# GpSimd's rotation of the next tile and its scaling of head norms, placed behind the last level of a recurrence tile

## The chip, the cores and the metric

The kernel runs on one core of a Trainium2 chip. The core has TensorE (PE in the profile, its weight loads PEld), VectorE (DVE), ScalarE (ACT), GpSimd (POOL), SyncE (SP) and 16 DMA engines. The metric is the device time of one execution of the whole program in microseconds, as the median over runs. The kernel before takes 2104.66 us (median of 3 runs, 2103.86 to 2107.75).

## What is computed

Two layers of a hybrid encoder over 1040 frames of a new stream and 32 frames of a running one. Each layer normalises its input, projects it with `w_in` into twenty slices, runs four groups of heads, and merges them with gates and `w_out`. Two of the four groups, HGRN2 and retention, are the gated linear recurrence below; retention's queries and keys are first rotated, and both outputs are normalised per head. This is the part around the change:

```python
q_d = _rope(heads(dq, H_D), pos)
k_d = _rope(heads(dk, H_D), pos) * (HD_D ** -0.5)
...
# _gla: S_t = diag(exp(logf_t)) S_{t-1} + k_t v_t^T,  o_t = S_t^T q_t, block by block
b = jnp.cumsum(gb, axis=1)
inter = jnp.einsum('bthk,bhkv->bthv', qb * jnp.exp(b), S)
att = jnp.einsum('bthk,bshk,btshk->bhts', qb, kb, decay)
intra = jnp.einsum('bhts,bshv->bthv', att, vb)
S_new = jnp.exp(b_end)[..., None] * S + jnp.einsum('bshk,bshv->bhkv', kb * jnp.exp(b_end[:, None] - b), vb)
...
def _head_rms(o):
    return (of * lax.rsqrt(jnp.mean(of * of, axis=-1, keepdims=True) + EPS)).astype(o.dtype)
```

The other two groups are forgetting attention and sparse attention. For the sparse one a threshold per query is found by a bitwise search over index scores, which VectorE does in many small pieces while other stages run.

## The kernel before, in words

Frames are cut into nine tiles of 128 (tile 0 holds the running stream and the 16 meta tokens, tiles 1 to 8 the 1024 frames). A layer runs in four stages: index scores with the first projections, the recurrence, the rest of the projections, and attention with the output projection. The order on each engine is the order of the code, and engines meet by semaphores only.

The recurrence goes tile by tile. For tile t TensorE makes the cumulative sums of the log decays (L1031, L1032), turns queries and keys (L1036, L1038 for HGRN2; L1046 for retention, which waits for `x_rope`), and then goes through the levels (L1067): `ret`, 0, and 1 to 7 (1 to 5 in tile 0). A level from 1 on is a product of queries and keys weighted with decays of its block size, so for each level VectorE makes a difference of sums (`dl`, L1848), ScalarE its exponentials (L1548, L1549), VectorE multiplies keys and queries with them (L1887 and twice L1890, releasing `x_ql`), TensorE multiplies (releasing `x_lv`), and VectorE copies the result under a mask into `attA` (L1868, L1872, releasing `x_cp`). Behind the levels TensorE makes outputs (L1085, L1090) and state updates (L1098); VectorE adds them to the states (L1920, releasing `x_s`).

Projection work fills the gaps. Between the steps of a tile TensorE runs `fill` (L927, L924), a number of matmul steps laid down by `UPTO`, and 8 steps are one job. ScalarE empties a finished job's bank (L1414, releasing `p_ev`) and stores it (L1420); the job after the next one needs that bank. VectorE fills its own gaps with `search`: the counts at L1783, and after each eight counts the small operations L1822, L1824, L1826 and L1817. Fifteen such steps belong to each tile from 1 on: 8 before L1840, 2 before the levels, 5 behind them.

GpSimd per tile: `clear` (L2161, a memset of `attA`), `decayed` (L2145, L2146, L2149), `forget(t + 1)` (L2130, L2132, L2136), `rotate(t + 1)` (L2115, L2116, L2120, L2121, L2123, releasing `x_rope`), and `normed_heads(t - 1)` (L2156, releasing `x_on`). ScalarE waits for `x_on` in `store_heads(t - 1)` (L1504), which stands in its order behind the exponentials of the last level. Behind it in ScalarE's order come the evacuations of jobs that end late in the tile (L1414), the copy of the outputs (L1563) and the first steps of the next tile (L1521, L1522, L1523, releasing `x_eb`).

Of the kernel before, what the change touches and what calls it, by code (L numbers as in the profile page):

```python
# [31 lines left out]
NT = 1 + SEQ // P  # L32
# [121 lines left out]
def steps(keys):  # L154

    return {k: i + 1 for i, k in enumerate(keys)}
# [7 lines left out]
def one_more(count):  # L164

    count[0] += 1
    return 1


def encoder(nc, ins, outs, cf_d, cb_d, cm_d, cf_at, cb_at, cm_at):  # L170
# [10 lines left out]
    with ctx:  # L181
# [5 lines left out]
        def sem(name):  # L187
            s = ctx.enter_context(nc.semaphore(name))
            all_sems.append(s)
            return s  # L190
# [7 lines left out]
        def C(name):  # L198
            return cf[:, slice(*cf_at[name])]
# [273 lines left out]
        def span(mu):  # L473
            cols = [(c, w) for _, w, c in pieces_of(mu)]
            return min(c for c, _ in cols), max(c + n for c, n in cols)
# [111 lines left out]
        LEV = [(t, j) for t in T_all for j in (["ret", 0] + list(range(1, 6 if t == 0 else 8)))]  # L587
# [49 lines left out]
        x_cp, x_cp_at = sem("x_cp"), steps(LEV)  # L637
# [46 lines left out]
        for layer in range(DEPTH):  # L684
# [10 lines left out]
            with nc.Block() as block:  # L695
# [658 lines left out]
                def copy_keys(copy, a, own_sem, own):  # L1354

                    _, m, u, j = a
                    b = tbank[a]
                    if m == "fox":
                        rows = NS if u == "s" and j == NCACHE else P
                        col = (P * j if u == "s" else max(0, width(u - 1))) if u != 0 else 0  # L1360
                        n_ = HALF if u == 0 else rows
                        return copy(foxKT[0:HD + 1, :, col:col + n_], ps[0:HD + 1, 512 * b:512 * b + 512].rearrange("p (h n) -> p h n", h=H)[:, :, 0:n_])
                    if u == "s":
                        n_ = min(SW - P * j, 4 * P)
                        return copy(dsaKT["s"][0:HD, P * j:P * j + n_], ps[0:HD, 512 * b:512 * b + n_])
                    if j == 0:
                        copy(dsaKT["p"][0:HD, 0:HALF], ps[0:HD, 512 * b:512 * b + HALF]).then_inc(own_sem, one_more(own))
                        return copy(dsaKT["p"][0:HD, HALF:HALF + 3 * P], ps[0:HD, 512 * b + P:512 * b + 4 * P])
                    n_ = min(NT - j, 4) * P
                    return copy(dsaKT["p"][0:HD, width(j - 1):width(j - 1) + n_], ps[0:HD, 512 * b:512 * b + n_])  # L1370
# [729 lines left out]
                def _(pool):  # L2100
# [7 lines left out]
                    def rotate(t):  # L2108

                        pool.wait_ge(ld_mix[ld_mix_slot[t]], ld_mix_at[t] * 2)  # L2110
                        cosv = C("cos")[:, t * half:(t + 1) * half][:, None, :].broadcast_to([P, 4 * H, half])
                        sinv = C("sin")[:, t * half:(t + 1) * half][:, None, :].broadcast_to([P, 4 * H, half])
                        qk = LD[t % 2][:, 0:2, :].rearrange("p a (h d) -> p (a h) d", d=half)
                        rp = rope[t % 2]
                        G.tensor_tensor(rc.rearrange("p a b c -> p (a b) c"), qk, cosv, ALU.mult).then_inc(pool_own, one_more(own))  # L2115
                        G.tensor_tensor(rs_.rearrange("p a b c -> p (a b) c"), qk, sinv, ALU.mult).then_inc(pool_own, one_more(own))  # L2116
                        pool.wait_ge(pool_own, own[0])
                        if t >= 2:
                            pool.wait_ge(x_su, x_su_at[t - 2])
                        G.tensor_tensor(rp[:, :, 0], rc[:, :, 0], rs_[:, :, 1], ALU.subtract).then_inc(pool_own, one_more(own))  # L2120
                        G.tensor_tensor(rp[:, :, 1], rs_[:, :, 0], rc[:, :, 1], ALU.add).then_inc(pool_own, one_more(own))  # L2121
                        pool.wait_ge(pool_own, own[0])
                        G.tensor_tensor(kendD[t % 2].rearrange("p (h d) -> p h d", h=H), rp[:, H:].rearrange("p h a d -> p h (a d)"),  # L2123
                                        C("gk0" if t == 0 else "gk1")[:, :, None].broadcast_to([P, H, HD]), ALU.mult).then_inc(x_rope, 1)

                    def forget(t):

                        f = sig[t % 2]
                        pool.wait_ge(x_sg, x_sg_at[t])
                        G.tensor_tensor(f, f, oml[:, :], ALU.mult).then_inc(pool_own, one_more(own))  # L2130
                        pool.wait_ge(pool_own, own[0])
                        G.tensor_tensor(f, f, lb[:, :], ALU.add).then_inc(pool_own, one_more(own))  # L2132
                        pool.wait_ge(pool_own, own[0])
                        if t >= 2:
                            pool.wait_ge(x_qk, x_qk_at[t - 2])
                        G.tensor_scalar(kA[t % 2], f, -1.0, 1.0, ALU.mult, ALU.add).then_inc(x_kf, 1)  # L2136

                    def decayed(t):

                        if t >= 1:  # L2140
                            pool.wait_ge(x_su, x_su_at[t - 1])
                        pool.wait_ge(x_eb, x_eb_at[t])
                        pool.wait_ge(x_qke, x_qke_at[t])
                        pool.wait_ge(x_kf, x_kf_at[t])
                        G.tensor_tensor(QbA, QKA[:, 0], expb, ALU.mult).then_inc(pool_own, one_more(own))  # L2145
                        G.tensor_tensor(kendA, kA[t % 2], kex, ALU.mult).then_inc(pool_own, one_more(own))  # L2146
                        pool.wait_ge(x_qkde, 2 * x_qkde_at[t])
                        pool.wait_ge(pool_own, own[0])
                        G.tensor_tensor(QbD, QKD[:, 0], C("gq0" if t == 0 else "gq1"), ALU.mult).then_inc(x_qb, 1)  # L2149

                    def normed_heads(t):

                        pool.wait_ge(x_hr, x_hr_at[t])
                        if t >= 1:
                            pool.wait_ge(st_on, 16 * t)
                        G.tensor_tensor(oN, oAD, hr[:, :, None].broadcast_to([P, 2 * H, HD]), ALU.mult).then_inc(x_on, 1)  # L2156

                    def clear(t):
                        if t >= 1:
                            pool.wait_ge(x_o, x_o_at[t - 1])  # L2160
                        G.memset(attA, 0.0).then_inc(x_zero, 1)  # L2161
# [14 lines left out]
                    for t in T_all:  # L2176
                        if t >= 1:
                            clear(t)
                        decayed(t)
                        if t + 1 < NT:  # L2180
                            forget(t + 1)
                            rotate(t + 1)
                        if t >= 1:
                            normed_heads(t - 1)
# [82 lines left out]
```

## Time and profile before

| | us |
|---|---|
| median of 3 runs | 2104.66 |
| the profiled execution, whole | 2108.83 |
| its span | 2107.0 |
| PE busy in the span | 1923.3 (91%) |
| DVE busy | 1387.2 (66%) |
| ACT busy | 736.7 (35%) |
| POOL busy | 254.4 (12%) |
| mean granted TensorE clock | 0.988 |

The profile is of one execution, and its span is the time from the first to the last instruction. The recurrence stage lies at 231 to 532 us in the first layer and at 1282 to 1583 us in the second, and a tile of it takes 32 to 34 us. Idle time of an engine is printed before the instruction that ended it, in brackets, with the instruction that released it.

### The profile page before, as it was taken

The page shows a single profiled execution, that of the slowest core. Times are in us where ns is not written, and L with a number is a line of the kernel's source. Part 1 is how long each engine was busy: PE and PEld are TensorE (multiplying, and loading weights), DVE is VectorE, ACT ScalarE, POOL GpSimd, SP SyncE. Part 2 cuts the span into 40 slices and gives each one's busy share as a digit, 9 for nine tenths or more (in the row PEclk, how much of TensorE's full clock was granted, in tenths as well). Part 3 has the DMA queues.
Part 4 walks back from the last instruction along what each step waited for, and adds up shares of the span by engine and source line. Part 5 has one row for each costly group of instructions (what it writes and reads, how often), then busy time and mean ns, then how long its engine had stood idle before and what let it go on. Part 6 is the DMA issues. An engine that isn't in the chain of part 4 may idle for free. (4 is left out here: it accounts for less than half of the span.)

```text
span 2107.0 us, 27058 instructions
## 1 busy us (share of the span) xinstructions
PE 1923.3 (91%) x9670; PEld 1073.9 (51%) x9690; DVE 1387.2 (66%) x2961; ACT 736.7 (35%) x1678; POOL 254.4 (12%) x361
## 2 busy tenths in 40 slices
PE   7999999999998888999779999999999987889997
PEld 6434466555445556544364344665554455565443
DVE  4469398989796666542234693989888956674322
ACT  4451233423113444433244512434331134344332
POOL 0000223322100000001100002234221000000011
PEclk9999999999999999999979999999999999999999
DMA  7102232130513002224251022331314130122242
GB/s 245 59 22 78 70 106 86 61 103 28 154 38 73 14 14 91 87 99 147 107 175 61 23 75 75 103 99 46 103 43 139 38 76 11 34 70 88 99 149 105
DMA packets 151156, 173.44 MB, mean 82 GB/s; under 512 B 71392, under 2 KB 106848, under 8 KB 150832
## 3 DMA queue, kind: packets, MB, share of 16 engines
q1 hardware_dynamic: 122960, 134.34, 20.4%
q10 hardware_dynamic: 28064, 37.38, 5.0%
q8 instruction: 78, 1.28, 0.2%
q14 instruction: 54, 0.44, 0.1%
HBM read 114.94 MB, written 62.24 MB: 84 GB/s over the span
## 5 line engine op out<-in xcount | busy, mean ns | idle before, releaser
L927 PE MATMUL ps<-wring,xnT_arena 128*128 128x512 f32 (+2 forms) x2304 | 920.3, 541 | 0.0
L927 PEld LDWEIGHTS ps<-wring,xnT_arena 128*128 128x128 f32 x2304 | 403.1, 191 | 355.7 <-issue 338.7
L1783 DVE TENSOR_SCALAR_CACHE_REDUCE arena<-arena,theta 32x1056 bf16<-32x1056 f32 x496 | 461.3, 979 | 2.3
L1414 ACT COPY arena<-ps 128x512 f32<-128x512 f32 (+3 forms) x144 | 75.3, 523 | 447.7 <-PE ps L927 414.1
L1291 PE MATMUL ps<-wring,xnT_arena 128*128 128x512 f32 x512 | 222.8, 593 | 0.0
L2067 DVE TENSOR_REDUCE mneg<-ps 128x1 f32<-128x192 f32 (+9 forms) x148 | 113.9, 770 | 84.6 <-PE ps L1223 82.1
L1291 PEld LDWEIGHTS ps<-wring,xnT_arena 128*128 128x128 f32 x512 | 95.9, 190 | 114.8 <-issue 114.8
L1067 PEld LDWEIGHTS ps<-arena 128*128 128x128 f32 x488 | 68.7, 190 | 103.5 <-DVE arena L1890 75.1
L1067 PE MATMUL ps<-arena 128*128 128x128 f32 x488 | 79.5, 286 | 35.9 <-DVE arena L1890 35.7
L2235 POOL TENSOR_TENSOR arena<-arena 128x1024 f32<-128x1024 f32 (+1 forms) x16 | 35.4, 2213 | 584.0 <-DVE arena L2008 397.5
L1378 ACT COPY xnT_arena<-ps 128x512 f32<-128x512 f32 (+3 forms) x84 | 39.0, 464 | 181.8 <-PE ps L1235 139.1
L1221 PE MATMUL ps<-xnT_arena,arena 128*128 128x512 f32 (+4 forms) x240 | 86.3, 475 | 14.8 <-DVE xnT_arena L1378 13.2
L1221 PE MATMUL ps<-arena 128*128 128x512 f32 (+4 forms) x240 | 92.6, 473 | 7.8 <-DVE xnT_arena L1378 6.7
L1890 DVE TENSOR_TENSOR arena<-o_bc,arena 64x128 f32<-64x128 f32 x244 | 95.7, 392 | 3.8
L1645 ACT ACTIVATE arena<-ps,mneg 128x576 f32<-128x576 f32 (+5 forms) x84 | 80.9, 963 | 25.1 <-DVE mneg L2067 24.4
L1378 DVE COPY xnT_arena<-ps 128x512 f32<-128x512 f32 x104 | 61.2, 605 | 38.7 <-PE ps L1271 20.4
L1766 DVE SCALAR_TENSOR_TENSOR arena<-arena,iw 32x1056 f32<-32x1056 f32 (+7 forms) x64 | 63.7, 996 | 27.8 <-ACT arena L1477 25.7
L1235 PE MATMUL ps<-cf,arena 128*128 128x128 f32 (+2 forms) x596 | 79.1, 273 | 1.0 <-ACT arena L1645 1.0
L1872 DVE COPY_PREDICATED arena<-cm,ps 128x256 f32<-128x256 uint8 x122 | 63.5, 521 | 23.6 <-PE ps L1067 22.4
L1848 DVE TENSOR_TENSOR arena<-arena 128x256 f32<-128x256 f32 x122 | 76.2, 635 | 2.7
L1548 ACT ACTIVATE arena<-arena 128x128 f32<-128x128 f32 x122 | 37.7, 309 | 106.5 <-DVE arena L1848 100.1
L1235 PEld LDWEIGHTS ps<-cf,arena 128*128 128x128 f32 (+2 forms) x596 | 63.9, 136 | 18.9 <-issue 12.8
(271 smaller groups left out, 2468.0 us busy)
## 6 DMA issues: line engine op xcount, KB each, us to landing
projected<-arena ACTq DMA_DIRECT2D x130, 256.0 KB, 2.0
wring<-in_w_in SPq DMA_DIRECT2D x16, 1024.0 KB, 7.8
o_bc<-projected SPq DMA_DIRECT2D x36, 384.0 KB, 3.7
wring<-in_w_in SPq DMA_DIRECT2D x6, 2048.0 KB, 9.0
arena<-residual SPq DMA_DIRECT2D x17, 512.0 KB, 5.1
arena<-in_x_prompt SPq DMA_DIRECT2D x16, 512.0 KB, 5.0
wring<-in_w_out SPq DMA_DIRECT2D x8, 1024.0 KB, 6.1
residual<-arena SPq DMA_DIRECT2D x16, 512.0 KB, 2.7
```

The costliest lines, as they stand in the source:

```text
L927: o = mm(bank(pbank(k), 0, w_), xnT[:, c, t * P:(t + 1) * P], w, start=(c == 0), stop=(c == CH - 1))
L1067: o = mm(bank(level_bank(k), 2 * n_ * g, 2 * n_), keys[:, g * P:(g + 1) * P], queries[:, g].rearrange("p e n -> p (e n)"), start=True, sto ...
L1221: o = mm(ps[:, col:col + w], qt[:, h, :], kt[:, h if m == "fox" else 0, key:key + w], start=True, stop=not adds, skip_group_check=True)
L1235: o = tr(ps[0:w, 512 * tbank[a] + P * i:512 * tbank[a] + P * i + P], pbuf((m, u, h))[:, col:col + w], C("ident"))
L1291: o = mm(bank(OUT_BANK[t] + half), yT[t % 2][:, c, :], wring[:, c * D + 512 * half:c * D + 512 * half + 512], start=(c == 0), stop=(c == C ...
L1378: copy(ptile[pt_of[m, u, h]][:, 4 * g * P:4 * g * P + size], bank(tbank[a], 0, size)).then_inc(te, 1)
L1414: nc.scalar.copy(stage[s][:, 0:wide], bank(pbank(k), 0, wide)).then_inc(p_ev, 1)
L1645: A(pbuf((m, u, h))[:, 0:hi - lo], ps[:, base + lo:base + hi], ACT.Exp, bias=mneg[:, s:s + 1], accum_out=rsum[:, s:s + 1]).then_inc(a_exp, 1)
L1783: V.tensor_scalar(cmp_out[0][r, (i % 2) * WMAX:(i % 2) * WMAX + uw[u]], score[u][r], th_, 0.0, op, ALU.add, accum_out=into[r, i:i + 1]).th ...
L1848: V.tensor_tensor(dl[k[1] % 2].rearrange("p (b s) -> p b s", s=size), bv, bv[:, :, size // 2 - 1:size // 2].broadcast_to([P, 2 * P // size ...
L1890: V.tensor_tensor(QL[k[1] % 2][r, :, e, :].rearrange("p g (b i) -> p g b i", i=size // 2), cut_(QKA[:, 0])[r, :, :, size // 2:], cut_(E[k[ ...
L2067: V.tensor_reduce(mneg[:, s:s + 1], ps[:, base + lo:base + hi], X, ALU.max, negate=True).then_inc(a_max, 1)
```

## The change

One wait is added to GpSimd's program. Behind `forget(t + 1)` GpSimd waits until the last level's result of tile t has been copied (`x_cp`), and only then rotates tile t + 1 and scales the head norms of tile t - 1. The instructions and their order stay as they are.

```diff
                         decayed(t)
                         if t + 1 < NT:
                             forget(t + 1)
+                        pool.wait_ge(x_cp, x_cp_at[[k for k in LEV if k[0] == t][-1]])
+                        if t + 1 < NT:
                             rotate(t + 1)
                         if t >= 1:
                             normed_heads(t - 1)
```

GpSimd's instructions in tile 0, the first place where the wait stands, with the semaphores that each waits for (`-` is the kernel before, `+` the changed one):

```order
 L2132 TENSOR_TENSOR arena<-arena,lb 128x256 [waits pool_own]
 L2136 TENSOR_SCALAR arena<-arena 128x256 [waits pool_own]
-L2115 TENSOR_TENSOR arena<-o_bc,cf 128x512 [waits ld_mix1]
+L2115 TENSOR_TENSOR arena<-o_bc,cf 128x512 [waits ld_mix1,x_cp]
 L2116 TENSOR_TENSOR arena<-o_bc,cf 128x512
 L2120 TENSOR_TENSOR arena<-arena 128x8x32 [waits pool_own]
```

The first multiplication of `rotate` now waits for `x_cp` as well, and what follows it on GpSimd waits with it. In tile 8, where nothing is left to rotate, the wait stands before the scaling of tile 7's head norms; GpSimd's rows there in the changed kernel:

```order
L2145 TENSOR_TENSOR arena<-o_bc,arena 128x256 [waits x_qke,x_kf,x_eb,x_su]
L2146 TENSOR_TENSOR arena<-arena 128x256
L2149 TENSOR_TENSOR arena<-o_bc,cf 128x256 [waits pool_own,x_qkde]
L2156 TENSOR_TENSOR arena<-arena,small 128x512 [waits st_on,x_hr,x_cp]
L2156 TENSOR_TENSOR arena<-arena,small 128x512 [waits st_on,x_hr]
```

Nothing has moved among the rows; the first L2156 (tile 7) has gained `x_cp`, the second (tile 8) waits for what it waited for before.

## Rows read from the trace of the kernel before

**Rows 1.** Costliest groups: line, engine, operation, count | busy us, mean ns | idle before, releaser.
```profile
L1067 PE MATMUL ps<-arena 128*128 128x128 f32 x488 | 79.5, 286 | 35.9 <-DVE arena L1890 35.7
```

**Rows 2.** Waits of PE, recurrence of the first layer: total us, times, longest.
```profile
PE ps L1067 <- DVE arena L1890: 18.0, 20, 2.0
```

**Rows 3.** Stretch, length, busy us (instructions) of PE, PEld, DVE, ACT, POOL; clock, DMA.
```profile
350.30:360.30 10.00, 7.66 (x30) 3.75 (x29) 9.75 (x22) 3.16 (x12) 7.25 (x9) 1.00 0.13 51
516.90:526.90 10.00, 9.95 (x48) 5.39 (x47) 8.30 (x25) 2.95 (x11) 1.04 (x1) 1.00 0.13 33
```

**Rows 4.** Timeline, levels of tile 3: start us, us, engine, line [idle before <-releaser].
```profile
352.05 1.12 POOL L2115 TENSOR_TENSOR arena<-o_bc,cf 128x512 f32<-128x512 f32 x1
352.27 0.71 PE L1067 MATMUL ps<-arena 128*128 128x128 f32 x4 [0.21 <-DVE arena L1890]
...
356.79 1.08 POOL L2156 TENSOR_TENSOR arena<-arena,small 128x512 f32<-128x512 f32 x1
356.90 1.44 DVE L1890 TENSOR_TENSOR arena<-o_bc,arena 64x128 f32<-64x128 f32 x2
...
358.39 0.71 PE L1067 MATMUL ps<-arena 128*128 128x128 f32 x4 [1.28 <-DVE arena L1890]
```

**Rows 5.** Timeline of PE, third level in tiles 6 and 7.
```profile
451.85 0.71 PE L1067 MATMUL ps<-arena 128*128 128x128 f32 x4 [0.82 <-DVE arena L1890]
...
485.60 0.71 PE L1067 MATMUL ps<-arena 128*128 128x128 f32 x4 [0.33 <-DVE arena L1890]
```

**Rows 6.** Timeline of DVE, from the last level of tile 3 to its states.
```profile
362.61 0.44 DVE L1872 COPY_PREDICATED arena<-cm,ps 128x256 f32<-128x256 uint8 x1 [0.86 <-PE ps L1067]
...
365.46 0.17 DVE L1822 TENSOR_TENSOR sel<-sel 128x8 f32<-128x8 f32 x1
...
367.86 0.47 DVE L1920 SCALAR_TENSOR_TENSOR s_hgrn<-s_hgrn,arena,ps 128x64 f32<-128x64 f32 x2 [0.27 <-PE ps L1098]
```

**Rows 7.** Timeline of POOL, a rotation with no VectorE work beside it (tile 0).
```profile
231.54 1.09 POOL L2115 TENSOR_TENSOR arena<-o_bc,cf 128x512 f32<-128x512 f32 x1 [60.22 <-DMA o_bc<-projected]
...
235.24 0.61 POOL L2123 TENSOR_TENSOR arena<-arena,cf 128x256 f32<-128x256 f32 x1
```

**Rows 8.** Timeline, search operations of DVE beside GpSimd's L2146 and L2202.
```profile
276.00 1.06 DVE L1783 TENSOR_SCALAR_CACHE_REDUCE arena<-arena,theta 128x832 bf16<-128x832 f32 x1
276.13 0.73 POOL L2146 TENSOR_TENSOR arena<-arena 128x256 f32<-128x256 f32 x1
...
561.19 0.26 DVE L1822 TENSOR_TENSOR sel<-sel 128x8 f32<-128x8 f32 x1
```

**Rows 9.** Timeline of DVE and PE, third level of tile 8.
```profile
517.73 0.60 DVE L1890 TENSOR_TENSOR arena<-o_bc,arena 64x128 f32<-64x128 f32 x2
...
518.54 0.61 PE L1067 MATMUL ps<-arena 128*128 128x128 f32 x4
```

**Rows 10.** Timeline, from the last level of tile 2 into tile 3.
```profile
327.90 0.44 ACTq L1504 DMA_DIRECT2D projected<-arena  x1
...
329.25 0.45 DVE L1872 COPY_PREDICATED arena<-cm,ps 128x256 f32<-128x256 uint8 x1 [1.02 <-PE ps L1067]
...
329.93 0.27 ACT L1414 COPY arena<-ps 128x132 f32<-128x132 f32 x1 [2.42 <-PE ps L927]
...
335.36 2.38 PE L924 MATMUL ps<-wring,xnT_arena 128*64 128x256 f32 x20
```

**Rows 11.** Timeline, from tile 3's outputs to tile 4's levels.
```profile
369.47 0.39 ACT L1523 ACTIVATE arena<-ps 128x256 f32<-128x256 f32 x1
...
374.31 0.60 PE L1046 MATMUL ps<-cf,arena 128*128 128x128 f32 x4
...
377.59 1.80 DVE L1848 TENSOR_TENSOR arena<-arena 128x256 f32<-128x256 f32 x2
```

**Rows 12.** Timeline of PE and DVE, from the recurrence to the start of attention.
```profile
539.53 48.23 PE L927 MATMUL ps<-wring,xnT_arena 128*128 128x512 f32 x112
...
649.41 1.46 DVE L1362 COPY xnT_arena<-ps 65x512 f32<-65x512 f32 x2 [5.29 <-PE ps L1137]
```

## Prediction, made before the changed kernel ran

> **What bounds the kernel now.** I read the page's engine shares first: TensorE is busy for 91% of the span, so the question is where it is idle in the stage that the change touches, and whether a gain there survives to the end. The costliest groups answer the first half: TensorE sat idle 35.9 us before the matmuls of the levels, and 35.7 us of that ended when VectorE's multiplication L1890 ended [rows 1]. The waits of the first layer's recurrence give 18.0 us in 20 waits [rows 2], which leaves 17.7 us for the second layer. So inside the levels VectorE is late, and TensorE waits.
>
> The table of busy times then shows when. In ten us of tile 3's levels GpSimd is busy for 7.25 us and TensorE for 7.66; in ten us of tile 8's levels, where GpSimd has nothing to rotate, GpSimd is busy for 1.04 us and TensorE for 9.95 [rows 3]. The timeline says how [rows 4]: GpSimd's rotation and scaling run from 352.05 to 357.87; the pair of L1890 takes 1.44 us beside them, where it takes 0.60 us in tile 8 [rows 9], and TensorE's idle time of 1.28 us ends as that pair ends.
>
> Second half: after the recurrence TensorE runs its projections in unbroken rows, the first of 48.23 us, and VectorE waits 5.29 us for it at the start of attention [rows 12]. The fill steps are fixed in number, so each us by which the last tile ends earlier moves the end of the projections, and VectorE's search is shifted with it (its steps per tile are fixed as well). A gain in the levels is kept in full.
>
> **The change part by part.** All instructions stay; only the moment of six GpSimd instructions per tile moves, from the levels to behind the last level.
>
> *What it removes.* Idle time of TensorE before L1067: 18.0 + 17.7 us [rows 1, 2]. Not all of it is due to the moved work. `forget` (L2130 to L2136) stays among the levels and delays VectorE just before the third of the numbered levels: 0.21 us in tile 3, whose wait ended at 352.27, only 0.22 us after the rotation began [rows 4]; 0.82 and 0.33 us in tiles 6 and 7 [rows 5]. Tiles 1 and 5 repeat tile 3's pattern. That is 3 x 0.21 + 0.82 + 0.33 = 1.8 us, and I take 2.0 us per layer since tile 7 is already a little late when its fourth level comes. Removed: 16.0 us in the first layer, 15.7 us in the second.
>
> Does something else become late at once? Without the moved work a level costs TensorE 1.3 or 2.2 us by turns (products and one or two fill steps), and VectorE about 1.5 us, so they are near balance. Tile 8 is the test: it runs so and shows no idle at its levels [rows 3]. So the gain per tile is TensorE's idle time, not VectorE's larger saving.
>
> *What it adds behind the levels, on VectorE.* The last level's copy of tile 3 ends at 363.05 [rows 6]. From there GpSimd rotates: 4.31 us when undisturbed [rows 7] (235.85 - 231.54), and L2156 adds 1.08 us [rows 4], 5.4 us in all, against 5.8 us among the levels. In this stretch VectorE counts. A count is not slowed by GpSimd: 1.06 us for 128x832 beside L2146 [rows 8]. The small operations behind eight counts can be: L1822 took 0.26 us instead of 0.17 beside a tiny GpSimd multiplication [rows 6, 8]. By the 15-step pattern they fall behind the levels in tiles 1, 3, 5 and 7. There L1822 would start at 365.46, while the rotation's third instruction (0.72 us long) runs, and I put 0.6 us each on L1822 and L1826 (what is left of that third instruction, and most of the fourth), 1.2 us in all; L1920 waits 0.27 us for TensorE anyway [rows 6], so VectorE enters the next, even tile 0.9 us late. How much of that TensorE feels depends on the room before its third level: 0.2 us in tile 8 (L1890 ends at 518.33, the matmul starts at 518.54) [rows 9], none in tile 6, which waits already [rows 5]; from the same two lines in the timeline about 0.4 us in tile 4 and 0.6 us in tile 2. Cost: 0.3 + 0.5 + 0.9 + 0.7 = 2.4 us per layer. Bounds: 0, if the small operations slip through between GpSimd's; 7 us, if all four wait 0.6 us (2.4 - 0.3 = 2.1 us late in four tiles, less the room of 1.2 us).
>
> The Trainium skill (SBUF — State Buffer, SBUF: two separate sides, and Who interferes with whom) says that VectorE and GpSimd share a port pair as an exclusive lock, which a VectorE instruction with two SBUF inputs needs against a GpSimd instruction that reads SBUF, and a `tensor_scalar` in a 2-port mode too, but not the form that writes its accumulator. The counts are of that last form, and the trace agrees (1.06 us beside GpSimd). By that rule L1824 and L1817 could be held as well, which is the upper bound just given and a rival below.
>
> *What it adds on ScalarE.* ScalarE now stands at L1504 until `x_on`, about 5.5 us behind the last level. Queued behind it are one evacuation, L1563 and L1521 to L1523. In tile 3 it would be free at 368.6, and with L1504's issue, L1414, L1420 and L1563 before it L1523 would end near 372 instead of 369.86 [rows 11]. VectorE first needs it at L1848, at 377.59 - so 5 us of room. `x_rope` comes 4.4 to 4.9 us behind the last level, at 368; L1046 takes it at 374.31 [rows 11]: 6 us of room. The bank of a late evacuation is wanted 8 steps later, 3 us or more of room with wide jobs. The exception is tile 2, whose jobs are narrow: the job evacuated at 329.93 must be out before the matmul at 335.36, 5.66 us after the last level's copy at 329.70 [rows 10]. New: 5.5 + 0.44 for the issue + 0.27 for the copy = 6.2 us, a stall of 0.6 us per layer (0 to 1.1). `clear`, the next GpSimd work, waits for outputs 4.2 us behind the last level, so it is at most 1.3 us later and is not wanted before the next levels.
>
> *The sum.* First layer 18.0 - 2.0 - 2.4 - 0.6 = 13.0; second 12.7; together 25.7 us. The profiled execution of 2108.83 us would take 2083.1; it lies 4.2 us over the median of 2104.66, so the median becomes 2079 us, 1.2% faster.
>
> **The rivals.**
> 1. *Nothing is given back.* The small operations slip through and no bank is late: 2 x 16 = 31.7 us, 2073. For it: one sample only of a held L1822, by 0.09 us. Against: L1890 shows how much a VectorE multiplication with both inputs in SBUF loses.
> 2. *VectorE is late in every even tile.* All four small operations are held: 7 us per layer in place of 2.4, so 31.7 - 14 - 1.2 = 16.5 us, 2088. For it: the lock of the rule above. Against: nothing in the trace shows a held `tensor_scalar`.
> 3. *The waits only change place.* VectorE was to be late anyway, and TensorE's idle time comes back at other levels: within 4 us of 2104.66. Against: tile 8 [rows 3].
> 4. *GpSimd becomes the bound, slower.* If the counts, which fill VectorE behind the levels, kept GpSimd from its reads, six instructions would take longer, and ScalarE, stuck at L1504, would hand out `x_eb` too late. The point is where the block passes 11 us (14.5 us from 363.05 to 377.59, less 3.5 us of ScalarE's work behind it). If each instruction took 2.5 times its time, the block would be 14.5 us, 3.5 us too long in 16 tiles, 56 us lost against 31.7 won: 2129. Against: L2146 beside a count takes its usual 0.73 us.
>
> **How the numbers follow.** My forecast, 25.7 us give or take 4, has a chance of 0.60; rival 1 0.16; rival 2 0.14; rival 3 0.05; rival 4 0.04; 0.01 for the rest. The range takes in the first three: from 2071 (rival 1 with both layers' last idle time gone too) to 2090. About 0.2% of the time (4 us) is what a measurement can tell from no change. Faster by more than that: 0.92. Within it: 0.04. Slower: 0.04.
>
> **What would show it.** In the changed profile: L1890's wait falls from 18.0 to about 5 us in a recurrence, what is left of it before the third level, larger in even tiles (2, 4, 6, 8) than in odd ones; L1822 and L1826 behind the last level of odd tiles take 0.5 to 0.8 us; L2115 starts some 0.1 us behind L1872; one wait of 0.6 us for L1414 stands before L924 in tile 3; a recurrence is 13 us shorter and the rest of the program keeps its length. I am wrong if idle time appears before L1046 or before the levels begin (rival 4), or if L1067 still waits more than 10 us per layer (rivals 2 and 3).

## The result, and the profile after

| | before | after |
|---|---|---|
| median, us (runs, lowest to highest) | 2106.20 (4, 2103.86 to 2109.53) | 2074.40 (4, 2072.01 to 2076.44) |
| the profiled execution, us | 2108.83 | 2073.58 |
| its span, us | 2107.0 | 2071.8 |
| mean granted TensorE clock | 0.988 | 0.989 |

The changed kernel takes 0.9843 of the time (95% interval 0.9827 to 0.9858), 31.8 us less. The forecast was 2079.0 in a range of 2071 to 2090. The time lies in the range, 4.6 us under the forecast, and nearer to rival 1 (2073) than to it. The profiled executions differ by 35.25 us where 25.7 was predicted. So the question of the experiments is where the rest came from, 6.1 us by the medians and 9.6 us by the profiled executions, and whether rival 1's reason (nothing given back) is the true one. It isn't.

The page of the kernel after: engine shares, the group that [rows 1] showed, and the group of L1890.

```profile
PE 1915.3 (92%) x9690; PEld 1075.4 (52%) x9690; DVE 1349.9 (65%) x2961; ACT 734.6 (35%) x1678; POOL 246.2 (12%) x361
...
L1067 PE MATMUL ps<-arena 128*128 128x128 f32 x488 | 77.2, 281 | 7.6 <-DVE arena L1890 7.6
...
L1890 DVE TENSOR_TENSOR arena<-o_bc,arena 64x128 f32<-64x128 f32 x244 | 73.5, 301 | 3.8
```

TensorE's idle time before L1067 fell from 35.9 us [rows 1] to 7.6. The 244 multiplications of L1890 take 301 ns each in place of 392 (before, the group read 95.7 us). Note too that L1067 itself is busy for 77.2 us in place of 79.5, though its matmuls are the same; that small difference turns out to be the key.

The waits of PE in the first layer's recurrence (after it lies at 231 to 520 us), which answer [rows 2]:

```profile
PE ps L1067 <- DVE arena L1890: 4.0, 12, 1.0
PE ps L1031 <- ACT arena L1494: 2.0, 1, 2.0
PE ps L924 <- ACT arena L1414: 0.5, 1, 0.5
```

18.0 us in 20 waits became 4.0 us in 12, and the predicted late bank is there as a wait of its own. Where the 4.0 us lie, from the timeline of PE after, one row each of tiles 3, 4, 6 and 8 (the other eight waits are 0.15 to 0.32 us):

```profile
342.95 0.71 PE L1067 MATMUL ps<-arena 128*128 128x128 f32 x4 [0.21 <-DVE arena L1890]
...
372.00 0.71 PE L1067 MATMUL ps<-arena 128*128 128x128 f32 x4 [0.43 <-DVE arena L1890]
...
436.79 0.71 PE L1067 MATMUL ps<-arena 128*128 128x128 f32 x4 [1.02 <-DVE arena L1890]
...
499.24 0.71 PE L1067 MATMUL ps<-arena 128*128 128x128 f32 x4 [0.30 <-DVE arena L1890]
```

Tile 3's wait of 0.21 us behind `forget` stayed, as in [rows 4]; tile 6's grew from 0.82 [rows 5] to 1.02; tile 8, which had none [rows 9], now has two.

Behind the last level of tile 3, the timeline of all engines after (the place of [rows 6]):

```profile
350.64 0.44 DVE L1872 COPY_PREDICATED arena<-cm,ps 128x256 f32<-128x256 uint8 x1 [0.86 <-PE ps L1067]
...
351.16 1.09 POOL L2115 TENSOR_TENSOR arena<-o_bc,cf 128x512 f32<-128x512 f32 x1 [8.40 <-DVE arena L1872]
...
353.39 0.73 POOL L2120 TENSOR_TENSOR arena<-arena 128x256 f32<-128x256 f32 x1
...
353.49 0.65 DVE L1822 TENSOR_TENSOR sel<-sel 128x8 f32<-128x8 f32 x1
...
354.08 0.72 POOL L2121 TENSOR_TENSOR arena<-arena 128x256 f32<-128x256 f32 x1
...
354.18 0.65 DVE L1824 TENSOR_SCALAR bitv<-sel 128x8 int32<-128x8 f32 x1
...
354.86 0.17 DVE L1826 TENSOR_TENSOR prefix<-prefix,bitv 128x8 int32<-128x8 int32 x1
...
355.06 0.47 DVE L1817 TENSOR_SCALAR theta<-prefix 128x8 int32<-128x8 int32 x1
```

L2115 starts 0.08 us behind L1872's end. L1822 ends 0.02 us behind the end of GpSimd's L2120, L1824 0.03 behind L2121's, and L1817 0.02 behind that of L2123 (354.88 to 355.51); L1826, which starts between L2121 and L2123, takes its usual 0.17. Three of the four small operations are held, by 0.48, 0.48 and 0.30 us, together 1.26 us, and the same in tiles 1, 5 and 7 and in the second layer.

For the lengths below I cut a recurrence at TensorE's first L1031, L1046 and L1085 of each tile. Only the stretch from L1046 to L1085, which holds the levels, changes in every tile:

| from L1046 to L1085, us, by tile | 0 | 1 | 2 | 3 | 4 | 5 | 6 | 7 | 8 | sum |
|---|---|---|---|---|---|---|---|---|---|---|
| before | 17.85 | 24.41 | 24.45 | 24.41 | 22.99 | 24.48 | 25.01 | 24.19 | 22.21 | 210.0 |
| after | 16.51 | 21.76 | 21.80 | 21.76 | 22.12 | 21.82 | 22.80 | 21.58 | 22.81 | 193.0 |

That is 17.0 us per layer, where the printed idle time before L1067 fell by 14.0. Tile 3 gives back 0.60 us for the late bank (6.61 to 7.21 us from L1031 to L1046). Net, a layer gains 16.4 us, and two layers 32.9, which agrees with the 31.8 us between the medians.

The whole recurrence was 18.1 us shorter in each layer of the profiled executions. The other 1.7 us are the clock: before, TensorE ran at half clock (0.51 granted, its level of 1.2 GHz) for 3.4 us at the start of tile 0, after 2.36 us of idle time before L1031. After, it ran the first 3.4 us of tile 0 at full clock, though it had been idle for 2.04 us. Tile 0 starts at 238.42 before and at 236.84 after; its first 3.4 us in the table of busy times, first of before, then of after:

```profile
238.40:241.80 3.40, 3.38 (x8) 2.30 (x9) 0.00 (x0) 0.94 (x3) 0.00 (x0) 0.51 0.00 0
```

```profile
236.84:240.24 3.40, 3.40 (x12) 2.00 (x13) 0.00 (x0) 1.47 (x4) 0.00 (x0) 1.00 0.00 0
```

Outside the recurrences the differences are partly in how long like matmuls took and partly in waits. Before the first recurrence 1.6 us were gained: 32 like matmuls of L924 near the start took 4.20 us before and 3.02 after, which no row explains, and the idle time before L1031 was 2.04 us in place of 2.36. The two stages between recurrence and attention kept their length to 0.01 us (59.79 and 57.33 us), as predicted. From the start of attention in the first layer to the second recurrence 4.4 us were lost. Some 2.0 of them are waits of TensorE: for a DMA before L1137 1.20 us in place of 0.45, and for VectorE before L1321 2.09 and 2.15 us in place of 1.56 and 1.47. The rest goes with half-clock stretches, which were 34.1 us long in all in place of 30.7 and fell at other places. Behind the second recurrence 1.8 us were gained, 0.5 of them in such waits. The sum is 2 x 18.1 + 1.6 - 4.4 + 1.8 = 35.2 us, against 35.25 measured. These outer waits go both ways: that for the DMA in the first layer was 0.36 to 1.57 us long in the runs below, so it can't be put down to the edit.

### The profile page after: what moved, and what is told of

Its sections match the earlier page's. It is cut to its first block and busy times, and to the rows that moved or that the text cites. A ratio compares the mean times of both kernels' runs of the same rounds, so it can differ in the third digit from the quotient of the medians.

```text
span 2071.8 us, 27094 instructions
## 1 busy us (share of the span) xinstructions
PE 1915.3 (92%) x9690; PEld 1075.4 (52%) x9690; DVE 1349.9 (65%) x2961; ACT 734.6 (35%) x1678; POOL 246.2 (12%) x361
## 3 DMA queue, kind: packets, MB, share of 16 engines
q8 instruction: 78, 1.28, 0.3%
## 5 line engine op out<-in xcount | busy, mean ns | idle before, releaser
L1414 ACT COPY arena<-ps 128x512 f32<-128x512 f32 (+3 forms) x144 | 75.3, 523 | 490.6 <-PE ps L927 381.0
L1067 PEld LDWEIGHTS ps<-arena 128*128 128x128 f32 x488 | 70.3, 191 | 67.9 <-DVE arena L1890 36.7
L1067 PE MATMUL ps<-arena 128*128 128x128 f32 x488 | 77.2, 281 | 7.6 <-DVE arena L1890 7.6
L1872 DVE COPY_PREDICATED arena<-cm,ps 128x256 f32<-128x256 uint8 x122 | 63.6, 522 | 29.7 <-PE ps L1067 28.3
L1766 DVE SCALAR_TENSOR_TENSOR arena<-arena,iw 32x1056 f32<-32x1056 f32 (+7 forms) x64 | 63.7, 996 | 27.8 <-ACT arena L1477 25.7
L1890 DVE TENSOR_TENSOR arena<-o_bc,arena 64x128 f32<-64x128 f32 x244 | 73.5, 301 | 3.8
L1991 DVE TENSOR_TENSOR o_bc<-ps,rinv 128x128 f32<-128x128 f32 (+1 forms) x72 | 20.9, 291 | 81.2 <-PE ps L1279 79.8
L924 PE MATMUL ps<-wring,xnT_arena 128*64 128x256 f32 (+2 forms) x576 | 66.1, 369 | 2.0 <-ACT arena L1414 1.1
```

The costliest lines, as they stand in the source:

```text
L924: o = mm(bank(pbank(k), 0, n)[HALF * i:HALF * (i + 1)], xnT[:, c, 0:HALF], w[:, n * i:n * (i + 1)], start=(c == 0), stop=(c == CH - 1), sk ...
L1067: o = mm(bank(level_bank(k), 2 * n_ * g, 2 * n_), keys[:, g * P:(g + 1) * P], queries[:, g].rearrange("p e n -> p (e n)"), start=True, sto ...
L1414: nc.scalar.copy(stage[s][:, 0:wide], bank(pbank(k), 0, wide)).then_inc(p_ev, 1)
L1890: V.tensor_tensor(QL[k[1] % 2][r, :, e, :].rearrange("p g (b i) -> p g b i", i=size // 2), cut_(QKA[:, 0])[r, :, :, size // 2:], cut_(E[k[ ...
```

## Experiments

Theory A: a stalled L1067 costs TensorE more than its printed idle time, and the give-back predicted from VectorE's late small operations is real. Rival B (rival 1 of the prediction): nothing is given back, the remaining idle time has another cause. Beside these the runs ask what of GpSimd's work it was that delayed VectorE, and whether the rest can be had.

The first four ran on one chip (kernel before there 2110.12 us, so the changed kernel would be 0.9843 x 2110.12 = 2077.0), the last four on one chip as well (before 2107.64, changed kernel 2074.5).

**Half of the change: head norms back among the levels.**

```diff
                             forget(t + 1)
+                        if t >= 1:
+                            normed_heads(t - 1)
                         pool.wait_ge(x_cp, x_cp_at[[k for k in LEV if k[0] == t][-1]])
                         if t + 1 < NT:
                             rotate(t + 1)
-                        if t >= 1:
-                            normed_heads(t - 1)
```

> The changed kernel with one part undone: the scaling of head norms (L2156, 1.08 us) stands behind forget and in front of the new wait, so it runs among the levels again; the rotation stays behind the last level. Theory (GpSimd's products among the levels hold VectorE's products, TensorE waits for those): one product of 1.08 us holds VectorE about 0.8 us in tiles 2 to 8, right behind forget, where VectorE is already late; TensorE's wait for L1890 grows from 4.0 us to 8 to 10 us in a recurrence, and the time lies 8 to 13 us over the changed kernel, 20 us or more under the kernel before. Rival (the gain comes from something else that the wait changes, such as ScalarE's later L1504): all of the change's gain or none of it, so 2074 or 2105 us.

Measured: 2083.34 us, ratio 0.9872 (0.9854 to 0.989). The wait of L1067 in the first recurrence:

```profile
PE ps L1067 <- DVE arena L1890: 6.0, 13, 1.0
```

The wait for L1414 before L924 is gone, since `x_on` comes early again. The direction is the expected one, the size is not: 6.3 us over the changed kernel where 8 to 13 were expected, and 6.0 us of waits where 8 to 10 were. One GpSimd instruction of 1.04 us among the levels costs the level stretches 4.8 us per layer (197.8 in place of 193.0), though the printed idle time grows by 2.0 us only.

**The other half: the rotation back among the levels.**

```diff
                             forget(t + 1)
-                        pool.wait_ge(x_cp, x_cp_at[[k for k in LEV if k[0] == t][-1]])
                         if t + 1 < NT:
                             rotate(t + 1)
+                        pool.wait_ge(x_cp, x_cp_at[[k for k in LEV if k[0] == t][-1]])
                         if t >= 1:
                             normed_heads(t - 1)
```

> The changed kernel with the other part undone: the rotation (five products, 4.3 to 4.8 us) runs among the levels as in the kernel before, and the new wait stands behind it, so only L2156 runs behind the last level. Theory: the rotation holds VectorE four times a tile; what goes is the piece of L1890 held by L2156. TensorE's wait for L1890 falls from 18.0 to 9 to 12 us in a recurrence; with some 0.3 us more per wait that goes, the time is 10 to 16 us under the kernel before. The gains of the two parts add up to about that of the change (31 us). Rival (it is the whole of the change or nothing): 2105 us.

Measured: 2097.91 us, ratio 0.9946 (0.9928 to 0.9965). The wait of L1067, and the stretch of tile 7 behind its longest wait (2.04 us) in the table of busy times:

```profile
PE ps L1067 <- DVE arena L1890: 13.0, 17, 2.0
```

```profile
481.80:485.20 3.40, 3.40 (x9) 1.69 (x8) 2.81 (x10) 1.02 (x4) 0.67 (x1) 0.59 0.00 0
```

The level stretches take 205.3 us, 12.3 more than after, of which 1.7 are the half clock in tile 7 (0.59 granted over the stretch; four fill matmuls take 2.98 us there in place of 1.88). The kernel before had the same wait of 2.04 us in tile 7 and kept its clock. So the rotation is worth 10.6 us per layer and the norms 4.8, together 15.4 of the 17.0: nearly additive. The time, 12.2 us under the kernel before, is as expected; the waits of 13.0 us are a little over the expected 9 to 12.

**Is it GpSimd's time or its reads? Two products added among the levels.** Two 128x512 multiplications of the shape of L2115 are added before the wait, with their result written to the rotation's own scratch, which `rotate` overwrites; the computation is unchanged.

```diff
                             forget(t + 1)
+                        if t + 1 < NT:
+                            pool.wait_ge(ld_mix[ld_mix_slot[t + 1]], ld_mix_at[t + 1] * 2)
+                            wide_cos = C("cos")[:, (t + 1) * half:(t + 2) * half][:, None, :].broadcast_to([P, 4 * H, half])
+                            wide_qk = LD[(t + 1) % 2][:, 0:2, :].rearrange("p a (h d) -> p (a h) d", d=half)
+                            for _ in range(2):
+                                G.tensor_tensor(rc.rearrange("p a b c -> p (a b) c"), wide_qk, wide_cos, ALU.mult).then_inc(pool_own, one_more(own))
+                                pool.wait_ge(pool_own, own[0])
                         pool.wait_ge(x_cp, x_cp_at[[k for k in LEV if k[0] == t][-1]])
```

> The changed kernel plus two GpSimd products of 128x512 per tile in front of the new wait, in tiles 0 to 7 (the first product of the rotation, made twice more; its result is overwritten by the rotation): 2.4 us of GpSimd work that reads two tensors, put back among the levels. Theory (the products hold VectorE): VectorE loses about 1.5 us per tile, TensorE 1 to 1.5 us of it, over 16 tiles 16 to 26 us over the changed kernel, near 2095 us. Rival (what counts is how long GpSimd is busy, whatever it does): the same as in memsets_added. Rival (GpSimd's work among the levels does no harm by itself): 2074 us.

Measured: 2093.95 us, ratio 0.9922 (0.9902 to 0.9943), 17 us over the changed kernel. Waits of L1067: 9.6 us in 18. Tile 3's timeline:

```profile
346.08 2.35 POOL L2187 TENSOR_TENSOR arena<-o_bc,cf 128x512 f32<-128x512 f32 x2
346.28 1.20 DVE L1848 TENSOR_TENSOR arena<-arena 128x256 f32<-128x256 f32 x1
...
347.93 0.66 DVE L1887 TENSOR_TENSOR arena<-o_bc,arena 128x128 f32<-128x128 f32 x1
...
349.16 0.71 PE L1067 MATMUL ps<-arena 128*128 128x128 f32 x4 [0.43 <-DVE arena L1890]
```

**The same time filled with writes only.** Four memsets of the same scratch in the same place.

```diff
                             forget(t + 1)
+                        if t + 1 < NT:
+                            for _ in range(4):
+                                G.memset(rc.rearrange("p a b c -> p (a b c)"), 0.0).then_inc(pool_own, one_more(own))
+                                pool.wait_ge(pool_own, own[0])
                         pool.wait_ge(x_cp, x_cp_at[[k for k in LEV if k[0] == t][-1]])
```

> The changed kernel plus four GpSimd memsets of 128x512 per tile in front of the new wait, in tiles 0 to 7 (into the rotation's scratch tile, which the rotation overwrites): 2.4 us of GpSimd work that only writes, at the place of products_added. Theory (it is GpSimd's reading that holds VectorE's products of two tensors): no loss, 2074 us give or take 3, and TensorE's wait for L1890 stays at 4 us in a recurrence. Rival (any busy GpSimd holds VectorE): as products_added, 16 to 26 us over the changed kernel.

Measured: 2077.29 us, ratio 0.9839 (0.9817 to 0.9862), the changed kernel's own. Waits of L1067: 4.0 us in 11. Tile 3's timeline:

```profile
345.64 2.27 POOL L2184 MEMSET arena<- 128x512 f32 x4
...
345.87 0.43 DVE L1848 TENSOR_TENSOR arena<-arena 128x256 f32<-128x256 f32 x1
...
346.74 0.32 DVE L1887 TENSOR_TENSOR arena<-o_bc,arena 128x128 f32<-128x128 f32 x1
```

GpSimd is busy for 2.27 and 2.35 us beside the same VectorE instructions. Beside reads L1848 takes 1.20 us and L1887 0.66; beside writes they take 0.43 and 0.32, nearly their undisturbed time. So GpSimd's busy time beside VectorE cost nothing; its reads did. The Trainium skill (SBUF — State Buffer, Who interferes with whom) states just this, that VectorE with two SBUF inputs is in the way of a GpSimd instruction that reads SBUF and not of one that only writes it, and these two runs agree.

**The late bank undone.** ScalarE stores the head norms one tile later, so that it no longer stands at L1504 behind the levels.

```diff
                         follow(UPTO[t, "qk"] - at_step[0])
+                        if t >= 2:
+                            store_heads(t - 2)
                         act.wait_ge(x_qkd, x_qkd_at[t])
...
-                            if i == 6 and t >= 1:
-                                store_heads(t - 1)
...
+                    store_heads(NT - 2)
                     follow(CH)
```

> The changed kernel with ScalarE's store_heads (L1504 in the changed kernel, which waits for x_on) moved behind the first steps of the next tile, so ScalarE no longer stands there until GpSimd is done. Theory: what ScalarE's standing costs is one late bank per layer, the 0.54 us wait for L1414 in front of L924 in tile 3. That wait is gone, the stretch from L1031 to L1046 of tile 3 falls from 7.21 to 6.61 us, and all other stretches keep their length within 0.1 us: 1.2 us in all, which the times can't tell. Rival (ScalarE's standing makes other steps late as well): the tiles' other stretches shrink too, 3 us or more in all.

Measured: 2074.72 us (2 runs), ratio 0.9844 (0.982 to 0.9867). The waits of PE in the first recurrence:

```profile
PE ps L1067 <- DVE arena L1891: 4.2, 11, 1.0
PE ps L1031 <- ACT arena L1494: 2.0, 1, 2.0
```

The wait before L924 is gone and tile 3 has its 6.61 us again, so the bank was the cause. The 0.6 us didn't reach the end: the levels of tiles 2 and 5 grew by 0.3 us each (21.80 to 22.11, 21.82 to 22.10), where all other stretches had been expected to keep their length; why they grew is not shown.

**The small operations let through.** On top of the last kernel, GpSimd's block waits in odd tiles until TensorE's state updates are out (`x_su`), which is behind the small operations.

```diff
                         pool.wait_ge(x_cp, x_cp_at[[k for k in LEV if k[0] == t][-1]])
+                        if t % 2 == 1:
+                            pool.wait_ge(x_su, x_su_at[t])
                         if t + 1 < NT:
                             rotate(t + 1)
```

> store_late, and in the odd tiles GpSimd waits for the state updates (x_su, 4.8 us behind the last level) before it rotates, so that VectorE's four small search operations there find it idle. Theory (L1822 to L1817, held behind the levels of odd tiles, make VectorE late in even tiles): these four take 0.17 us each again, VectorE is about 1.5 us earlier in tiles 2, 4, 6 and 8, TensorE's waits there fall from about 2.7 us to 1 us in a layer, and the recurrence is 1.5 to 3 us shorter than in store_late; 4 to 7 us under the changed kernel with the late bank. Rival (the small operations are held but VectorE has room for it): the recurrence keeps its length, and only the 1.2 us of the late bank are won.

Measured: 2071.78 us, ratio 0.9832 (0.9817 to 0.9846). Waits of L1067: 2.7 us in 7. The levels of tile 4 fall from 22.13 to 20.56, of tile 6 from 22.82 to 22.38, of tile 8 from 22.83 to 21.69, and of tile 2 stay at 22.12; nothing changes in odd tiles' levels, and all four small operations take 0.17 us there again. So VectorE's late start into even tiles was real, and cost 3.1 us per layer in three of the four tiles. Rival B falls here. The time missed its expectation, 2.8 us under the changed kernel where 4 to 7 were expected. (Against the kernel without this wait the two intervals overlap; the finding rests on the trace.) The clock may have taken much of the gain: see the next run.

**`forget` behind the levels too.** On top of the same store, but without the wait for `x_su`: `forget` goes behind the wait for `x_cp`, and ScalarE makes its input (`log_forget`) behind the level loop.

```diff
                         decayed(t)
+                        pool.wait_ge(x_cp, x_cp_at[[k for k in LEV if k[0] == t][-1]])
                         if t + 1 < NT:
                             forget(t + 1)
-                        pool.wait_ge(x_cp, x_cp_at[[k for k in LEV if k[0] == t][-1]])
                         if t + 1 < NT:
                             rotate(t + 1)
...
-                            if i == 4 and t + 1 < NT:
-                                log_forget(t + 1)
                         follow(UPTO[t, "o"] - at_step[0])
+                        if t + 1 < NT:
+                            log_forget(t + 1)
```

> store_late, and forget (L2130, L2132, L2136, 2.1 us) goes behind the last level too, in front of the rotation, with ScalarE's log_forget (L1494) behind the levels. Theory (what is left of TensorE's waits in odd tiles, before the third level, is forget's): the waits in tiles 1, 3, 5 and 7 go, tile 6 loses its 0.8 us; tiles 2, 4, 8 stay late through the small operations, since GpSimd is busy 7.6 us behind the levels. The recurrence is 2 to 4 us shorter than in store_late, the whole 5 to 9 us under the changed kernel. Rival (the decays of the next tile now come too late): idle time of TensorE before L1031 in every tile, 1 us or more each, and the kernel is slower than the changed one by 10 us or more.

Measured: 2074.57 us, ratio 0.9846 (0.983 to 0.9863): no gain in time, and the expectation missed. The recurrence did get shorter in the trace, but by 2.2 us per layer only: tiles 1 to 5 and 7 gained 0.2 to 0.8 us each, tile 8 lost 0.6. The waits in the odd tiles are gone, as expected, but those in tiles 6 and 8 add up to 1.1 and 1.2 us, where they were 1.0 and 0.6. Behind the last level of tile 3:

```profile
351.50 1.10 POOL L2116 TENSOR_TENSOR arena<-o_bc,cf 128x512 f32<-128x512 f32 x1
351.83 0.78 DVE L1823 TENSOR_TENSOR sel<-sel 128x8 f32<-128x8 f32 x1
...
352.65 1.02 DVE L1825 TENSOR_SCALAR bitv<-sel 128x8 int32<-128x8 f32 x1
...
353.91 0.59 DVE L1818 TENSOR_SCALAR theta<-prefix 128x8 int32<-128x8 int32 x1
```

(From here the lines in search, levels and GpSimd's steps are one higher: L1823 is L1822, L1891 is L1890.) The wider instructions L2116 and L2117 now meet the small operations, which are held for 0.61, 0.85 and 0.42 us, 1.9 us in all in place of 1.26. A step taken out of one place had pushed the block onto the next. That even the 2.2 us per layer don't show in the time is most likely a matter of the clock: in its profiled execution TensorE ran 60.5 us at half clock, in that of the kernel with the late store 46.9 (60.6 in the run before this one, 47.2 in the changed kernel). 13.6 us more at half clock can cost up to 6.8 us, more than the 4.5 us by which the two recurrences got shorter. The mean granted clock was 0.985 in all four executions, and 0.986 to 0.989 in those of the changed kernel. The extra stretches lie behind the second recurrence (22.9 us at half clock there in this kernel, 9.4 in that with the late store). Why is open.

**Both together.** `forget` behind the levels (with the late store and `log_forget` placed as in the last run), and in odd tiles the wait for `x_su` between `forget` and `rotate`.

```diff
                         decayed(t)
+                        pool.wait_ge(x_cp, x_cp_at[[k for k in LEV if k[0] == t][-1]])
                         if t + 1 < NT:
                             forget(t + 1)
-                        pool.wait_ge(x_cp, x_cp_at[[k for k in LEV if k[0] == t][-1]])
+                        if t % 2 == 1:
+                            pool.wait_ge(x_su, x_su_at[t])
                         if t + 1 < NT:
                             rotate(t + 1)
```

> All of it: forget directly behind the last level, the rotation at once in even tiles and behind the state updates in odd tiles, store_heads late. Theory: no GpSimd product of two tensors but those of decayed stands beside the levels, and none beside the small operations; TensorE waits less than 1 us for L1890 in a recurrence, and a recurrence is 4 to 6 us shorter than in the changed kernel: 8 to 12 us in all, 2063 to 2067 us where the changed kernel takes 2075. Rival (TensorE and VectorE are so near balance that the last waits only move): less than 4 us under the changed kernel.

Measured: 2062.36 us (4 runs, 2061.73 to 2062.5), ratio 0.9785 (0.977 to 0.9799), 12 us under the changed kernel (8 to 12 expected) and the fastest of all. The page's group of L1067, the waits in the first recurrence, and tile 3's small operations:

```profile
L1067 PE MATMUL ps<-arena 128*128 128x128 f32 x488 | 74.9, 276 | 0.6 <-DVE arena L1891 0.5
```

```profile
PE ps L1067 <- DVE arena L1891: 0.3, 1, 0.3
```

```profile
352.41 0.17 DVE L1823 TENSOR_TENSOR sel<-sel 128x8 f32<-128x8 f32 x1
352.61 0.17 DVE L1825 TENSOR_SCALAR bitv<-sel 128x8 int32<-128x8 f32 x1
...
354.85 1.10 POOL L2116 TENSOR_TENSOR arena<-o_bc,cf 128x512 f32<-128x512 f32 x1 [2.75 <-PE ps L1098]
```

With nearly every product of GpSimd out of the way of VectorE's multiplications and small operations (one L1825 in tile 4 is still held, for 0.17 us), 35.9 us of idle time before L1067 [rows 1] have become 0.6.

## Why the prediction was right, and where it was short

**What bounds the kernel: right.** VectorE was late inside the levels because of GpSimd. The runs with products and with memsets show the cause, which the prediction only inferred from 1.44 against 0.60 us [rows 4, 9].

**A gain is kept in full: right as far as the start of attention.** The two stages behind the recurrence kept their length to 0.01 us. Behind them waits and clock moved by some us in both directions, as told above, and no run ties that to the edit.

**What the change removes: the price of a wait was too small.** This is the term that failed. The prediction took the printed idle time, 16.0 us per layer. Read how a stalled level differs from one in time, in tile 3 of the kernel after:

```profile
341.72 1.02 PE L927 MATMUL ps<-wring,xnT_arena 128*128 128x512 f32 x2
342.95 0.71 PE L1067 MATMUL ps<-arena 128*128 128x128 f32 x4 [0.21 <-DVE arena L1890]
343.50 1.88 PE L927 MATMUL ps<-wring,xnT_arena 128*128 128x512 f32 x4
...
345.66 1.02 PE L927 MATMUL ps<-wring,xnT_arena 128*128 128x512 f32 x2
346.52 0.61 PE L1067 MATMUL ps<-arena 128*128 128x128 f32 x4
346.97 1.88 PE L927 MATMUL ps<-wring,xnT_arena 128*128 128x512 f32 x4
```

In time, L1067 starts 0.86 us behind the start of the fill's 1.02 us (the rows overlap by 0.16), and the next fill starts 0.45 us later. Stalled, it starts 1.23 us behind (1.02 + 0.21) and the next fill 0.55 us later. So the wait printed as 0.21 costs 0.37 + 0.10 = 0.47 us, 0.26 more than printed, and the stalled group shows as 0.71 us in place of 0.61 whether idle time is printed or not. The rows of the weight loads (PEld) show what is lost. First the group at 342.95, then the group at 346.52:

```profile
342.95 0.52 PEld L1067 LDWEIGHTS ps<-arena 128*128 128x128 f32 x4 [1.04 <-DVE arena L1890]
...
346.18 0.19 PEld L1067 LDWEIGHTS ps<-arena 128*128 128x128 f32 x1 [0.32 <-DVE arena L1890]
```

The loads wait for L1890 as well. In time, the first of them are loaded 0.34 us before the matmul, beside the fill; stalled, their load starts with it. In both recurrences of all ten kernels every group of 0.71 us has its first load at its own start (within 0.04 us), and every group of 0.61 us has it 0.11 to 0.43 us earlier. There were 26 such groups in the first recurrence before (20 with printed idle time) and 14 after. 14.0 + 12 x 0.26 = 17.1 us; measured 17.0. The same rule, with the 0.26 of this one pair of levels and starting from the changed kernel, gives the level stretches of the other runs:

| first recurrence | printed idle, us | groups of 0.71 us | level stretches by the rule | measured |
|---|---|---|---|---|
| before | 18.0 | 26 | 210.1 | 210.0 |
| after | 4.0 | 14 | (start) | 193.0 |
| norms among the levels | 6.0 | 25 | 197.9 | 197.8 |
| rotation among the levels | 13.0 | 20 | 203.6 | 205.3 |
| products added | 9.6 | 24 | 201.2 | 201.0 |
| memsets added | 4.0 | 14 | 193.0 | 193.1 |
| bank undone | 4.2 | 15 | 193.5 | 193.6 |
| small operations let through | 2.7 | 9 | 190.4 | 190.5 |
| `forget` behind | 2.7 | 10 | 190.7 | 191.4 |
| both together | 0.3 | 3 | 186.4 | 186.7 |

It holds within 0.3 us but for two. In the run with the rotation the clock accounts for 1.7 us. The 0.7 us of `forget` behind the levels stay open.

**`forget` leaves 2.0 us: right.** After, tiles 1, 3 and 5 wait 0.21 to 0.22 us, tile 7 0.63 in two waits, and 0.82 of tile 6's 1.02 were there before: 2.1 us.

**VectorE late in even tiles, 2.4 us: the size nearly right, the instructions and the split not.** Forecast were L1822 and L1826, 0.6 us each, 1.2 us in all; held were L1822, L1824 and L1817, for 1.26 us in all. The sentence that nothing in the trace shows a held `tensor_scalar` was true of the trace and no ground to expect none: L1824 is one, and took 0.65 us. The rule of the Trainium skill (SBUF — State Buffer, Who interferes with whom) that I had put only into the upper bound and a rival, that a `tensor_scalar` other than the form with the accumulator can contend with GpSimd, was borne out by L1824 and L1817. What was printed in even tiles, beyond tile 6's old 0.82, is 0.16 in tile 2 (forecast 0.3), 0.89 in tile 4 (0.5), 0.20 in tile 6 (0.9) and 0.59 in tile 8 (0.7): 1.8 us in place of 2.4. In stretches it was worth 3.1 us, by the run that let the small operations through.

**The late bank, 0.6 us: right.** It stands before L924 in tile 3, on ScalarE's row L1414 behind L1504; timeline after:

```profile
325.21 0.33 ACTq L1504 DMA_DIRECT2D projected<-arena  x1
...
325.64 0.27 ACT L1414 COPY arena<-ps 128x132 f32<-128x132 f32 x1 [8.05 <-PE ps L927]
...
326.05 2.38 PE L924 MATMUL ps<-wring,xnT_arena 128*64 128x256 f32 x20 [0.54 <-ACT arena L1414]
```

Undoing it gave nothing in the sum of a layer, though, since other levels grew by as much.

**The sum.** First layer, predicted 16.0 - 2.4 - 0.6 = 13.0; in the terms as printed it was 14.0 - 0.6 = 13.4, and with the 3.1 us (12 x 0.26) that no row prints as idle 16.5 (measured 16.4). That the even tiles' cost above is 3.1 us too is chance. Both layers: 26 predicted, 33 measured. The remaining 2.4 us of the 35.25 are the differences told above, some 3.5 us gained where like matmuls ran faster and 1.2 us lost in waits outside the levels; nothing on record ties them to the edit. Counted from the kernel before as the result has it, 2106.20 us, the forecast would have been 2080.5 and the miss 6.1 us; 1.5 us of the nearness is luck.

**The rivals.** Rival 1 named the right time with the wrong reason: the give-back was there (3.1 us), and a larger gain than counted hid it, so that its time came out right by luck. Rival 2 had three of its four held operations, but the even tiles lost 3 us and not 7. Rivals 3 and 4 did not happen: the idle time did not come back, and there was none before L1046.

## What to carry to other kernels

A wait of TensorE that vanishes is worth its printed idle time and the overlap around it, which the trace shows if the distance between the starts of the rows is compared with a level that did not wait. Place GpSimd's products beside VectorE work other than the kinds that were held here, two-input operations on SBUF and the small `tensor_scalar` without an accumulator; the counts, which write an accumulator, lost nothing here, and the few tiny operations between them are what to steer the block around. When work is moved, look at what it meets at its new place: the wait past the small operations alone gave 3 us by the medians and moving `forget` alone nothing, and the two together 12. And compare the time at half clock of two profiles before a few us between them are explained.

## What was unexpected of the hardware

- An L1067 group that had to wait takes 0.71 us and not 0.61, and the start-to-start distance grows by 0.26 us beyond the idle time printed. Its first weight load starts with it, and not 0.11 to 0.43 us before.
- A 128x8 `tensor_scalar` from fp32 to int32 (L1824) takes 0.17 us alone, and 0.65 or 1.02 us beside GpSimd's `tensor_tensor` operations; a `tensor_tensor` on 128x8 int32 (L1826) right behind it took 0.17 us both times, having started in the gap between two GpSimd instructions.
- GpSimd itself lost less: L2115 took 1.09 us alone and 1.12 to 1.27 us among the levels of the kernel before, L2116 1.09 and up to 1.28.
- The half clock of 3.4 us at the start of a recurrence (0.51 granted, 1.2 GHz) came in both layers of the kernel before, in neither of the changed one, and in one of the two of most others (the second of each of the last four kernels), with 1.96 to 2.53 us of idle time before it each time. Recurrences that started at full clock had 1.98 to 2.33 us before them, so the length of the idle time doesn't tell the two apart. In the run with the rotation it came in tile 7 of both layers behind 2.04 us of idle time that in the kernel before had cost no clock. What decides it is open; each costs 1.7 us.
